# A causal mask written into the score banks by ScalarE, and probabilities scaled by two broadcast products

## The reference, cut to what matters

```python
def masked_softmax(s, mask):
    s = jnp.where(mask, s.astype(jnp.float32), -jnp.inf)
    m = jnp.max(s, axis=-1, keepdims=True)
    ...
    e = jnp.where(mask, jnp.exp(s - m), 0.0)
    return e / jnp.maximum(jnp.sum(e, axis=-1, keepdims=True), 1e-30)
...
    s_s = jnp.einsum('bqgrh,bgqkh->bqgrk', qg, ks) * scale
    p_s = masked_softmax(s_s, m_s[:, :, :, None, :])
    o_s = jnp.einsum('bqgrk,bgqkh->bqgrh', p_s.astype(vs.dtype), vs)
...
    s_w = jnp.einsum('bqgrh,bkgh->bqgrk', qg, kw) * scale
    p_w = masked_softmax(s_w, m_w[None, :, None, None, :])
    o_w = jnp.einsum('bqgrk,bkgh->bqgrh', p_w.astype(vw.dtype), vw)
    g = gates.reshape(bn, qb, N_KV, GROUP, 3)
    o = g[..., 0:1] * o_c + g[..., 1:2] * o_s + g[..., 2:3] * o_w
```

## Time and profile before

| | |
|---|---|
| time, median of 3 runs (lowest to highest) | 772.97 us (772.43 to 774.43) |
| span of the profiled execution | 770.6 us |
| the execution's time beside its span | not measured apart; the median is 2.4 us above the span |
| TensorE busy | 750.7 us, 97% |
| VectorE busy | 566.9 us, 74% |
| ScalarE busy | 404.7 us, 53% |
| GpSimd busy | 130.8 us, 17% |
| in 147.0 to 158.7 us: TensorE, VectorE, ScalarE busy | 11.4, 10.8 and 7.0 of 11.7 us |

### The profile page before, as it was taken

How to read it: one execution, slowest core, us unless ns; L and a number is a source line. 1 busy time by engine, 2 the same in 40 slices (tenths; PEclk the granted TensorE clock), 3 DMA queues, 4 the chain that set the end, 5 groups by cost and what they waited for, 6 DMA issues and landing times.

```text
span 770.6 us, 16973 instructions
## 1 busy us (share of the span) xinstructions
PE 750.7 (97%) x6302; PEld 703.4 (91%) x6302; DVE 566.9 (74%) x1015; ACT 404.7 (53%) x805; POOL 130.8 (17%) x222
## 2 busy tenths in 40 slices
PE   8999999999999999999999989999999999999994
PEld 7997898988889999999869989988988999999993
DVE  4475689998779575665774687999977876766676
ACT  5544277666556444444445455865655563444452
POOL 2331014331100033100600000444011000000033
PEclk9999999999999999999999999999999999999998
DMA  8988456666845688765528774666667455656531
GB/s 315 295 286 263 127 165 182 204 220 220 293 161 169 187 249 276 239 175 181 167 87 249 236 228 146 196 191 208 220 231 282 129 176 185 181 176 189 174 129 56
DMA packets 42938, 154.94 MB, mean 201 GB/s; under 512 B 6640, under 2 KB 7664, under 8 KB 42096
## 3 DMA queue, kind: packets, MB, share of 16 engines
q1 hardware_dynamic: 33952, 115.55, 47.9%
q0 software_dynamic: 8912, 38.37, 14.9%
HBM read 145.77 MB, written 13.34 MB: 206 GB/s over the span
## 4 chain that ended last, share of the span: by engine, by line
PE 84%; DVE 11%; issue 2%; DMA 2%; ACT 1%; SPq 0%; DVEq 0%
PE bank L732 22%; PE bank L733 22%; PE bank L734 22%; PE bank L750 4%; DVE w_lo L1305 2%; PE bank L960 2%; DMA ring<-weights_dram 2%; DVE probs L1520 2%; PE bank L743 1%; PE bank L1001 1%; PE bank L901 1%; DVE probs_t L1535 1%; PE bank L895 1%; PE bank L931 1%; DVE u_max L1495 1%
## 5 line engine op out<-in xcount | busy, mean ns | idle before, releaser
L732 PE MATMUL bank<-x_hi,w_hi 128*128 128x264 f32 x1208 | 350.1, 290 | 1.4 <-DVE w_lo L1305 1.4
L1305 DVE TENSOR_TENSOR w_lo<-ring,w_hi 128x1024 fp32r<-128x1024 f32 x202 | 247.9, 1228 | 136.1 <-ACT w_hi L1103 132.4
L734 PE MATMUL bank<-x_lo,w_hi 128*128 128x264 f32 x1208 | 342.7, 284 | 0.0
L733 PE MATMUL bank<-x_hi,w_lo 128*128 128x264 f32 x1208 | 342.4, 283 | 0.0
L1103 ACT ACTIVATE w_hi<-ring 128x1024 fp32r<-128x1024 f32 x202 | 213.9, 1060 | 54.8 <-DMA ring<-weights_dram 27.1
L732 PEld LDWEIGHTS bank<-x_hi,w_hi 128*128 128x128 f32 x1208 | 227.6, 188 | 5.6 <-issue 3.3
L733 PEld LDWEIGHTS bank<-x_hi,w_lo 128*128 128x128 f32 x1208 | 227.8, 189 | 0.4
L734 PEld LDWEIGHTS bank<-x_lo,w_hi 128*128 128x128 f32 x1208 | 226.8, 188 | 0.0
L732 PE MATMUL bank<-h_rounded,w_hi 128*128 128x264 f32 x352 | 100.3, 285 | 0.2
L733 PE MATMUL bank<-h_rounded,w_lo 128*128 128x264 f32 x352 | 100.2, 285 | 0.0
L1155 ACT ACTIVATE h<-bank 128x264 f32<-128x264 f32 x88 | 35.1, 398 | 75.6 <-PE bank L734 70.0
(11 more groups left out here) (273 smaller groups left out, 1052.4 us busy)
## 6 DMA issues: line engine op xcount, KB each, us to landing
ring<-weights_dram SPq DMA_DIRECT2D x208, 512.0 KB, 4.0
cache_a<-kcmp_dram POOLq DMA_DIRECT2D x32, 128.0 KB, 4.1
cache_b<-vcmp_dram POOLq DMA_DIRECT2D x32, 128.0 KB, 3.9
cache_a<-ksel_dram POOLq DMA_DIRECT2D x32, 128.0 KB, 3.3
cache_b<-vsel_dram POOLq DMA_DIRECT2D x32, 128.0 KB, 3.2
kwin_out_dram<-kwin_dram POOLq DMA_DIRECT2D x8, 512.0 KB, 4.1
vwin_out_dram<-vwin_dram POOLq DMA_DIRECT2D x8, 512.0 KB, 6.0
cache_a<-kwin_dram POOLq DMA_DIRECT2D x2, 2048.0 KB, 11.4
```

The source lines that it names most:

```text
L732: pe.matmul(out, w_high[:, k0 + k, :], high, start=(k == 0), stop=False)
L733: pe.matmul(out, w_rest[:, k0 + k, :], high, start=False, stop=False)
L734: ins = pe.matmul(out, w_high[:, k0 + k, :], rest, start=False, stop=(k == kn - 1))
L1305: dve.tensor_tensor(w_lo[:, slot % RING], ring[:, slot % RING], w_hi[:, d % HI_RING].bitcast(F32), ALU.subtract).then_inc(w_lo_ready, 1)
```

## The change

1. **TensorE.** Except for the first pair of each layer, the three mask products go. The score products of those pairs no longer start a sum but add to what stands in the bank, and each bank is announced as soon as its own last score product is done.
2. **ScalarE.** After the four exponentials of a unit it waits for its own last one (`exped`), then writes the mask into the unit's late bank (512 columns: zeros and the causal table, for both branches, from the new table `late_seed`), and after the odd unit also into bank 7. These writes, not the exponentials, now mark the banks as emptied. The last pair of a layer writes nothing and only raises the semaphores.
3. **VectorE.** Scaling waits for `exped`, and is two products with a broadcast factor (512 and 256 elements) in place of four scalings.
4. **GpSimd** fills `late_seed` once at the start (a memset and a copy).

```diff
@@ GpSimd, at the start
+            pool.memset(late_seed[:, 0:P], 0.0)
+            pool.tensor_copy(late_seed[:, P:2 * P], c("causal"))
             pool.tensor_copy(causal_b[:, :], c("causal"))
...
@@ TensorE, scores
-                                      k_of[:, 2 * br + gp, 0:2 * P], start=(br == 0 and part == 0), stop=False,
-                                      skip_group_check=True)
+                                             k_of[:, 2 * br + gp, 0:2 * P], start=(i == 0 and br == 0 and part == 0),
+                                             stop=(i > 0), skip_group_check=True)
...
-                            late_scores(0, 1, part)
+                            ins = late_scores(0, 1, part)
+                        if i:
+                            done(ins, step, i, 0)
                         pe.wait_ge(early_odd, l * PAIRS + i + 1)
                         for part in range(3):
-                            late_scores(1, 1, part)
-                            early_scores(0, part)
+                            ins_late, ins_early = late_scores(1, 1, part), early_scores(0, part)
+                        if i:
+
+                            done(ins_late, step, i, 1)
+                            done(ins_early, step, i, 2)
+                            continue
                         for g2 in range(2):
                             masked(late[g2], late[g2][:, :].rearrange("p (a n) -> p a n", a=2)[:, :, P:2 * P], g2)
@@ ScalarE, exp
-                            if j:
-                                emptied_by(ins, "scores", p, g2)
-                            elif g2:
-                                emptied_by(ins, "scores", p, 2)
+                        ins.then_inc(exped, 1)
+                        act.wait_ge(exped, l * HEADS + i + 1)
+                        if p < PAIRS - 1:
+                            seeds = late_seed[:, :].unsqueeze(1).to_broadcast([P, 2, 2 * P])
+                            emptied_by(act.activation(late.rearrange("p (a n) -> p a n", a=2), seeds, ACT.Copy),
+                                       "scores", p, g2)
+                            if g2:
+                                emptied_by(act.activation(bank[MI][:, :].rearrange("p (a n) -> p a n", a=4),
+                                                          c("causal").unsqueeze(1).to_broadcast([P, 4, P]), ACT.Copy),
+                                           "scores", p, 2)
+                        else:
+                            act.sem_inc(emptied[FILL[l, "scores", p, g2][0]], 1)
...
@@ VectorE, scale
-                        wait_emptied(dve, l, "scores", i // 2, i % 2)
+                        dve.wait_ge(exped, l * HEADS + i + 1)
...
-                        at = 0
-                        for j, n in enumerate((256, 256, 128, 128)):
-                            ins = dve.tensor_scalar(probs[:, i % 2, at:at + n], probs[:, i % 2, at:at + n],
-                                                    u_fac[:, i % 2, j:j + 1], None, ALU.mult)
-                            at += n
+                        for at, n in ((0, 2 * P), (4 * P, P)):
+                            part = probs[:, i % 2, at:at + 2 * n].rearrange("p (a n) -> p a n", a=2)
+                            of = at // (2 * P)
+                            ins = dve.tensor_tensor(part, part, u_fac[:, i % 2, of:of + 2].unsqueeze(2).to_broadcast(
+                                [P, 2, n]), ALU.mult)
```

More of the change, by code:

```diff
@@ L324, in trunk @@
         ident_b = sb("ident_b", [P, P], BF16)
+        late_seed = sb("late_seed", [P, 2 * P])
         ones = sb("ones", [P, P])
@@ L441, in trunk @@
         early_odd = sem("early_odd_scores")
+        exped = sem("exped")
         k_hi_ready, k_split = sem("k_hi_ready"), sem("k_split")
@@ L894, in late_scores @@
                             q_of, k_of = factors(slice(g2 * HD, g2 * HD + HD), part)
-                            pe.matmul(late[g2][:, br * 2 * P:(br + 1) * 2 * P], q_of[:, P:2 * P],
-                                      k_of[:, 2 * br + gp, 0:2 * P], start=(br == 0 and part == 0), stop=False,
-                                      skip_group_check=True)
+                            return pe.matmul(late[g2][:, br * 2 * P:(br + 1) * 2 * P], q_of[:, P:2 * P],
+                                             k_of[:, 2 * br + gp, 0:2 * P], start=(i == 0 and br == 0 and part == 0),
+                                             stop=(i > 0), skip_group_check=True)
                         def early_scores(g2, part):
@@ L902, in early_scores @@
                                              q_of[:, 0:P], k_of[:, gp:gp + 3:2, 0:P],
-                                             start=(g2 == 1 and part == 0), stop=False, skip_group_check=True)
+                                             start=(i == 0 and g2 == 1 and part == 0), stop=(i > 0),
+                                             skip_group_check=True)
                         def masked(bank_, parts, j):
@@ L1215, in _ @@
                                                      accum_out=u_sum[:, g2, col:col + 1])
-                            if j:
-                                emptied_by(ins, "scores", p, g2)
-                            elif g2:
-                                emptied_by(ins, "scores", p, 2)
+                        ins.then_inc(exped, 1)
[10 more added lines that the diff above has]
+                            act.sem_inc(emptied[FILL[l, "scores", p, g2][0]], 1)
+                            if g2:
+                                act.sem_inc(emptied[FILL[l, "scores", p, 2][0]], 1)
                     elif step == "turn":
```

## The result

The changed kernel takes 788.91 us (787.81 to 789.11) against 773.36 us for the kernel before on the same chip: a ratio of 1.0194, 95% interval 1.0167 to 1.0221, and 15.6 us between the medians. Both are medians of four executions; the ratio is estimated from all of them and so isn't exactly the quotient of the medians. The profiled execution spans 786.0 us; before it was 770.6.

A forecast was written before the change was run, and what follows sets the result against it. It took a loop through VectorE and ScalarE in the score stage to decide the time, lengthened by ScalarE's seeds and waits. Layers' 8.56 + 8.05 gave +16.6 on 772.97, so 789.6 us, range 779 to 798.

The forecast's parts named there:

- The loop: Score stage, VectorE and ScalarE: maximum, exp, w_hi, w_lo, scale, next maximum; from 9.72 to 11.64 us.
- u: Start of a pair's first maximum on VectorE (L1489), from which the prediction counts times and periods.
- X: ScalarE's added time per pair: three seeds of 0.50 and two waits of 0.20, 1.90 us; ends 1.16 and 2.32.
- Pool work behind `pv_out`: VectorE's pool pieces before the next maximum, adding to the period: 1.32, 1.05 and 1.44 in pairs 1, 3, 4.
- The sum: Layer 0's seven periods between first maxima: 84.47 us against 75.44, so +9.03.
- TensorE's spare: Pair 7's second turn, layer 0: it started 0.47 us later than VectorE required, so TensorE feels 8.56 of 9.03.
- Layer 1: Its score stage: the same 84.47 us against 75.99, less 0.43, so +8.05 felt by TensorE.
- turn into wait: TensorE, 14 pairs: the 6.3 us saved by removing mask products become waiting for VectorE and gain nothing.
- The product saving arrives: Rival: TensorE's 6.3 us of removed mask products shorten the kernel to 766.7 us; chance 0.03.
- VectorE bounds: Rival: ScalarE hides its seeds and VectorE sets the pace, -1.4 us together, 770.1 us; chance 0.03.
- The point where the sign turns: Rival of no change: ScalarE's added 0.6 us per pair would leave the time around 773 us; chance 0.04.
- TensorE's clock falls: Rival: waits of 1.5 to 3 us per pair halve TensorE's clock, some +8 us per pair hit; chance 0.03.

The follow-up runs named there:

- run 5: Kernel before plus one line: ScalarE waits for the end of its own exp in each of 32 steps, nothing seeded; 774.07 us, ratio 1.0004.
- run 4: Changed kernel with mask writes (seeds) of 256 columns in place of 512, half of each bank keeping old contents; 780.04 us, ratio 1.0093.
- run 3: Changed kernel with the mask products of all pairs put back, the first score product overwriting each seed; 789.44 us, ratio 1.0216.
- run 6: Kernel before without the mask products of 14 pairs and without seeds, so those scores stay unmasked; 771.29 us, ratio 0.9977.
- run 7: Kernel before with one scaling in place of four, with the mask products 769.26 us, without those of 14 pairs 762.99 us.
- run 1: Kernel before with two broadcast products in place of the four scalings, mask products kept, no seeds; 773.03 us, ratio 1.0002.
- run 2: Changed kernel with the four scalings put back, seeds kept, mask products gone; 787.85 us, ratio 1.0191.

## Why the prediction was right

It said 789.6 us, with VectorE's and ScalarE's loop as the cause; the chip gave 788.91, 0.7 less. The difference tells more: +16.6 was forecast, and the medians differ by 15.6 and the profiled spans by 15.4. Part of the closeness is luck, since the kernel before now has a median of 773.36 where the sum started from 772.97.

- **The loop.** Predicted 9.72 + 0.02 + 1.90 = 11.64, found 11.57. ScalarE's w_hi starts 1.91 later after u, the seeds and waits as summed; w_hi itself took 1.04 where it took 1.11, so w_lo is only 1.84 later. Of X, the seeds were 0.54, 0.54 and 0.52 (predicted 0.50 each) and the waits 0.13 and 0.16 (predicted 0.20 each): two small errors of opposite sign. Run 5 priced the wait by itself at 0.15, run 4 the seeds by their width. That all of X arrived doesn't follow from pair 4 alone: in plain pairs the loop had 0.46 to spare (run 5), so from 10.18 they grew by 1.39, less than X, and only the new period of 11.57 is the loop's.
- **Pair 0**: predicted 10.82, found 10.83. **Pool work behind `pv_out`**: predicted 1.32, 1.05 and 1.44; found 1.32, 1.06 and 1.06. The third was the term that was mis-sized: I carried over the 0.80 of L1558 in pair 4, and the same instruction took 0.43 this time. Of its eight executions before, six took 0.42 or 0.43 and two 0.80, in pair 4 of each layer. Both times a copy of GpSimd ran beside it, which at 164.51 in the changed kernel it doesn't:

```profile
158.93 0.58 POOL L637 COPY state<-pu_one 128x480 f32<-128x480 f32 x1
```

In all traces together the instruction takes 0.80 six times, each time with this copy started 0.06 before it, and never otherwise.

- **The sum** was to be 84.47 and is 83.71: 0.38 of the difference is that pool piece, six times 0.07 nearly all the rest. TensorE's spare of 0.47 held: u of pair 7 is 7.87 later and its turn 7.41.
- **Layer 1**: predicted +8.05 felt, found 575.67 - 560.33 - (489.42 - 481.38) = 7.30 (560.33 is that turn's start in the kernel before). Between the stages another 0.63 came, 8.04 - 7.41. In the profiles of all the runs that stretch takes from 297.2 to 301.4 us, so this can't be told from chance.
- **The mask products**: "turn into wait" was right, and runs 3, 6 and 7 show it from three sides: worth nothing with the seeds, 2.0 us without them, 6.3 us once VectorE was lighter. Not all of it turned into wait: part went into TensorE's slower clock (run 3). For run 6 I had expected 2.3 to 2.8 and a sum near 74.2; the medians gave 2.0, the profile 74.7.
- **The products for scalings**: predicted +0.02 per unit, found 1.03 against 1.01 in rows and no change in run 1. By the Trainium skill ("VectorE: DVE Perf Modes", Mode 2×_2P and Side-by-side) I had estimated +0.09; the rows go against that estimate. By the Trainium skill ("ScalarE: Activation LUTs", What ACT_TABLE_LOAD costs) a seed was estimated at 0.61 long and 0.52 apart; the trace has 0.60 and 0.54, and agrees.
- **What was off in the signs**: VectorE waited 0.4 to 1.33 for w_hi in a pair, where I had said 1.5 to 2, and 0.58 for q_split where I had said 0.7. TensorE waited before the second turn 11 times, not 14, and by 0.2 to 2.2 us, with only three of them above 1.5: in the early pairs its own work still fills the period, and where its clock fell it needed the wait. I had also priced only bank 7's seed against the next scores. The row below shows a late bank's seed holding them up in pair 0, once in each layer. It cost nothing that shows, since before the second turn of pair 1 (118.37) TensorE waits for VectorE again, by 0.24:

```profile
112.35 0.35 PE L905 MATMUL bank<-z_rounded 64*128 64x256 f32 x1 [0.86 <-ACT bank L1231]
```

- **The rivals.** "The product saving arrives" falls with run 3, "VectorE bounds" with the periods of 11.57 and run 4. The point where the sign turns, X = 0.6, was not tested: run 5 has X = 0.3 but keeps the mask products, and no run of the change has an X between 0 and 1.2. The formula for it also leaves out VectorE's own 10.18 in plain pairs. At X = 0 it gives a layer's sum of 72.0, where run 6 has 74.7 and 75.5. "TensorE's clock falls" did happen, for 3.3 us and not for whole pairs, and cost nothing; see below.

## What to carry to other kernels

Before moving work to an idle engine, find the loop that sets the period and ask on which side of it the idle time lies. Against the kernel with neither mask products nor seeds (run 6), three ACTIVATEs and two waits between the maximum and w_hi cost some 17 us, 1.0194 less 0.9977 of 773; the same three behind w_hi, on the same engine, cost about 2, which is what the removed products had saved. A saving on the engine with 84% of the chain is worth what the stage's next bound leaves of it, here a third; take the instructions out without any replacement first, and see what there is to win.

## What the runs showed of the hardware

**TensorE's clock fell once in each layer.** In the kernel before the granted clock is 1.00 in every two microseconds of both stages. In the changed kernel, from 166 us on (window, its length, busy time and instructions of PE, PEld, DVE, ACT and POOL, then granted clock, DMA share, GB/s):

```profile
166.00:168.00 2.00, 0.00 (x0) 0.00 (x0) 1.97 (x4) 1.11 (x6) 0.00 (x0) 1.00 0.61 166
168.00:170.00 2.00, 1.90 (x12) 1.90 (x13) 1.38 (x3) 1.97 (x8) 0.96 (x2) 0.72 1.13 358
170.00:172.00 2.00, 2.00 (x11) 2.00 (x11) 1.86 (x8) 1.97 (x10) 0.00 (x0) 0.50 0.61 262
172.00:174.00 2.00, 2.00 (x20) 1.64 (x21) 1.27 (x4) 2.00 (x4) 0.00 (x0) 0.93 0.00 0
```

TensorE had been idle for 2.15 us before 168.10, ran at full clock again, and at 168.86 fell to half, 1.2 GHz. Its dense products with 264 columns start every 0.22 us there, in place of 0.12:

```profile
169.26 0.42 PE L738 MATMUL bank<-x_lo,w_hi 128*128 128x264 f32 x1
169.48 0.42 PE L736 MATMUL bank<-x_hi,w_hi 128*128 128x264 f32 x1
```

At 172.12 it was back. The same fall stands in layer 1 behind the wait at 539.88, in run 2 behind two waits of 2.12 (155.18 and 540.26), and in run 4 once, behind one of 2.08 (545.90). It does not follow each such wait: the 2.15 before 155.47 in the changed kernel had none after it, nor had the 1.92 before 164.43 in run 4. In run 3, where TensorE has the mask products and its waits stay at 1.8, and in every other run, there is none in the stages. It cost no time here, since the next maximum was 11.57 us after the last one, as in run 3 without a fall: TensorE was so far ahead of the loop that the slower stretch only used up its next wait. In a stage that TensorE bounds, the same stretch would cost about 1.6 us by my estimate, half of the 3.3 it lasted.

**A wait for one's own ACTIVATE with an accumulator read is cheap**: 0.13 to 0.16 us more from start to start, and in run 5, where it is done 32 times, nothing measurable in the time of the kernel.

**One instruction of VectorE takes nearly twice as long beside a copy of GpSimd**: L1558, 128x256 fp32, took 0.80 us beside the 0.58 us copy L637 and 0.42 or 0.43 in every execution without it. No run moved the copy on purpose, so that it is the cause is likely and not shown.
